# Depthwise convolution of 4 channel groups: one group as ScalarE products and GpSimd additions, 15 taps of another on TensorE, 78 taps on VectorE

## The reference

```python
def conformer_conv_group(a, gate, w_dw, b_dw, ln_g, ln_b):
    u = a * jax.nn.sigmoid(gate)
    k = w_dw.astype(u.dtype)[:, None, :]
    v = lax.conv_general_dilated(
        u, k, window_strides=(1,), padding=[(CONV_WIDTH - 1, 0)],
        dimension_numbers=("NWC", "WIO", "NWC"),
        feature_group_count=C_CONV) + b_dw.astype(u.dtype)
    v = layernorm(v, ln_g, ln_b)
    return jax.nn.silu(v)
...
        z = xn @ w_in[l] + b_in[l]
        a = z[..., :C_CONV]
        gate = z[..., C_CONV:2 * C_CONV]
        p = z[..., 2 * C_CONV:]
        y_conv = conformer_conv_group(a, gate, w_dw[l], b_dw[l], ln_g[l], ln_b[l])
        y_pool = multiscale_pool_group(p, w_pool[l], s_pool[l])
        y = jnp.concatenate([y_conv, y_pool], axis=-1)
        h = h + y @ w_out[l]
```

## Time and profile before

| | |
|---|---|
| median of 3 runs | 2058.88 us (2054.29 to 2060.63) |
| the profiled execution | 2058.82 us |
| its span in the profile | 2057.0 us |
| mean granted TensorE clock | 0.984 |
| PE busy | 1903.9 us, 93% of the span |
| DVE busy | 686.4 us, 33% |
| ACT busy | 467.6 us, 23% |
| POOL busy | 32.6 us, 2% |

### The profile page before, as it was taken

One profiled execution on the slowest core, in us unless ns is written; L12 is line 12 of the kernel. 1 busy time (PEld: TensorE's weight loads), 2 busy tenths in 40 slices (PEclk: granted clock), 3 DMA queues, 4 the chain that ended last, 5 costly groups with the idle time before them and its releaser, 6 DMA issues.

```text
span 2057.0 us, 20381 instructions
## 1 busy us (share of the span) xinstructions
PE 1903.9 (93%) x8678; PEld 1121.0 (54%) x8678; DVE 686.4 (33%) x944; ACT 467.6 (23%) x686; POOL 32.6 (2%) x41
## 2 busy tenths in 40 slices
PE   5989989999879999998888999988999999999998
PEld 5876766557644333343433334342344478888887
DVE  6474465376421110212011021201039742322234
ACT  5347545312211000010100001010030432222223
POOL 0000000000000000000000000000040000000000
PEclk9999999999989999999999999999999999999999
DMA  8211101386679999999999999999970105332311
GB/s 303 83 43 60 62 22 41 141 297 237 252 299 421 421 421 421 421 421 422 421 421 421 421 421 421 422 421 422 411 243 23 41 32 163 103 98 87 103 62 41
DMA packets 127551, 513.42 MB, mean 250 GB/s; under 512 B 7907, under 2 KB 62307, under 8 KB 77155
## 3 DMA queue, kind: packets, MB, share of 16 engines
q1 hardware_dynamic: 123088, 487.95, 59.8%
q10 hardware_dynamic: 4374, 24.18, 3.1%
HBM read 510.00 MB, written 2.10 MB: 249 GB/s over the span
## 4 chain that ended last, share of the span: by engine, by line
PE 69%; DMA 21%; DVE 6%; ACT 2%; issue 1%; SPq 0%; POOL 0%; ACTq 0%; DVEq 0%; POOLq 0%
PE ps L1147 10%; DMA work<-in_w_exp_up 9%; PE ps L1102 7%; DMA ring<-in_w_exp_up 7%; PE ps L1315 5%; PE ps L537 5%; PE ps L1275 4%; PE ps L1276 4%; PE ps L1274 4%; PE ps L553 3%; PE ps L555 3%; PE ps L1025 3%; PE ps L554 3%; PE ps L1128 2%; PE ps L736 2%; PE ps L1048 1%
## 5 line engine op out<-in xcount | busy, mean ns | idle before, releaser
L1102 PE MATMUL ps<-work 128*64 128x512 f32 x1208 | 329.6, 595 | 28.6 <-DMA work<-in_w_exp_up 28.4
L1102 PE MATMUL ps<-ring,work 128*64 128x512 f32 x712 | 218.5, 594 | 19.6 <-DMA ring<-in_w_exp_up 19.5
L1102 PEld LDWEIGHTS ps<-work 128*64 128x64 f32 x1208 | 104.5, 137 | 207.5 <-issue 150.2
L2250 DVE TENSOR_TENSOR work<-work,ps 64x512 f32<-64x512 f32 x64 | 44.3, 692 | 449.0 <-ACT work L1687 448.4
L1687 ACT ACTIVATE work<-ps 64x512 f32<-64x512 f32 x64 | 37.7, 589 | 563.4 <-PE ps L1102 563.4
L537 PE MATMUL ps<-work,ring 128*128 128x512 f32 x320 | 138.9, 592 | 0.7 <-issue 0.7
L1274 PE MATMUL ps<-xh,wh 128*128 128x512 f32 x352 | 137.0, 389 | 0.0
L1276 PE MATMUL ps<-xh,wl 128*128 128x512 f32 x352 | 136.9, 389 | 0.0
L1275 PE MATMUL ps<-xl,wh 128*128 128x512 f32 x352 | 136.9, 389 | 0.0
L1102 PEld LDWEIGHTS ps<-ring,work 128*64 128x64 f32 x712 | 67.7, 137 | 125.8 <-issue 88.6
L2383 DVE TENSOR_TENSOR wl<-ring,wh 128x2048 fp32r<-128x2048 f32 x33 | 75.6, 2292 | 179.9 <-ACT wh L1775 179.9
(11 more groups left out here) (344 smaller groups left out, 2583.7 us busy)
## 6 DMA issues: line engine op xcount, KB each, us to landing
work<-in_w_exp_down SPq DMA_DIRECT2D x78, 1024.0 KB, 26.5
work<-in_w_exp_gate SPq DMA_DIRECT2D x76, 1024.0 KB, 26.8
work<-in_w_exp_up SPq DMA_DIRECT2D x75, 1024.0 KB, 27.0
ring<-in_w_exp_up SPq DMA_DIRECT2D x45, 1024.0 KB, 27.1
ring<-in_w_exp_gate SPq DMA_DIRECT2D x44, 1024.0 KB, 26.7
ring<-in_w_exp_down SPq DMA_DIRECT2D x43, 1024.0 KB, 27.0
ring<-in_w_in SPq DMA_DIRECT2D x27, 1024.0 KB, 6.3
work<-in_ada_w ACTq DMA_DIRECT2D x16, 1024.0 KB, 6.1
```

Of the source, the lines that this page charges most:

```text
L1102: i = e.matmul(PS[64 * gu:64 * gu + 64, fb, :], at(XET + 128 * k + 64 * z, 64), flat(key)[:, 512 * fb:512 * fb + 512], start=(k == 0), sto ...
```

## The change

`DVE_TAPS = 16` is the number of taps of group 1 that stay on VectorE.

- Group 3 leaves TensorE. ScalarE makes each of its 31 products, tap 0 with the bias straight into `CV + 1536`, the others into four rooms of 512 columns (`tap_room`) used in turn. GpSimd adds tap 1 to tap 30 to the sum, one after the other. `cv_m` counts the products and `cv_g` what GpSimd has done: first the weight tiles, then the additions. A product of tap k above 4 waits for addition k - 4.
- Group 1: taps 0 to 15 stay on VectorE, taps 16 to 30 are made on TensorE in bank 6, after dense blocks 8 and 9. VectorE adds the bank to its own sum as its 79th step. GpSimd makes 15 weight tiles.
- On TensorE, dense blocks 8 and 9 now stand ahead of the taps and block 10 ahead of the mean. On ScalarE the third `pool_in` now stands ahead of the squares, and the products stand behind the sigmoids.
- `pool_window` has an additional wait for the window before it.

```diff
+        def tap_room(k):
+
+            return at(DG + 2048 + 512 * (k % 4), 512)
+
+        CV_G = 31 - DVE_TAPS + 30
...
             glu(3, 1, 2, 0)
-            e.wait_ge(s["gl_u"], 1)
+            pool_dense(8, 3, 5)
+            pool_dense(9, 2, 5)
+            e.wait_ge(s["gl_u"], 4)
             e.wait_ge(s["pads"], 1)
             e.wait_ge(s["x_ca"], 63)
-            for k in range(31):
-                e.wait_ge(s["dg"], k + 1)
-                p = e.matmul(bank(6), at(DG + 128 * k, 128), at(U + 542 * 3 + k, 512), start=(k == 0), stop=(k == 30))
+            for k in range(DVE_TAPS, 31):
+                e.wait_ge(s["cv_g"], k - DVE_TAPS + 1)
+                p = e.matmul(bank(6), at(DG + 128 * (k - DVE_TAPS), 128), at(U + 542 + k, 512), start=(k == DVE_TAPS), stop=(k == 30))
             p.then_inc(s["cv_pe"], 1)
-            pool_dense(8, 3, 5)
-            pool_dense(9, 2, 5)
+            pool_dense(10, 1, 4)
             e.wait_ge(s["x_ym"], 32)
             for i in (3, 2, 0, 1):
                 if i == 3:
-                    e.wait_ge(s["cv_a"], 1)
+                    e.wait_ge(s["cv_g"], CV_G)
                 else:
-                    e.wait_ge(s["cv_d"], {2: 44, 0: 78, 1: 93}[i])
+                    e.wait_ge(s["cv_d"], {2: 44, 0: 78, 1: 79}[i])
                 p = e.matmul(bank(4), cst("o512"), at(CV + 512 * i, 512), start=(i == 3), stop=(i == 1))
             p.then_inc(s["ln_pe"], 1)
-            pool_dense(10, 1, 4)
...
+            def tap_3(k):
+
+                w = at(O_VEC + VEC["wdw"][0] + 93 + k, 1)
+                if k == 0:
+                    e.wait_ge(s["gl_u"], 1)
+                    e.wait_ge(s["pads"], 1)
+                    e.activation(at(CV + 1536, 512), at(U + 542 * 3, 512), ACT.Identity, bias=vcol("bdw", 3), scale=w).then_inc(s["cv_m"], 1)
+                    return
+                if k > 4:
+                    e.wait_ge(s["cv_g"], 31 - DVE_TAPS + k - 4)
+                e.activation(tap_room(k), at(U + 542 * 3 + k, 512), ACT.Copy, scale=w).then_inc(s["cv_m"], 1)
...
                 e.activation(at(TP + 512 * m, 512), bank(2 * m % 4), ACT.Sigmoid, bias=vcol("bin", 4 + i)).then_inc(s["gl_sg"], 1)
+                for k in range(*((0, 5), (5, 13), (13, 21), (21, 31))[m]):
+                    tap_3(k)
...
-            conv((0, 14, 31), (1, 0, 17))
-            conv((1, 17, 31))
+            conv((0, 14, 31), (1, 0, DVE_TAPS))
+            e.wait_ge(s["cv_pe"], 1)
+            e.wait_ge(s["cv_d"], done[1])
+            e.tensor_tensor(at(CV + 512, 512), at(CV + 512, 512), bank(6), ALU.add).then_inc(s["cv_d"], 1)
...
-            for k in range(31):
-                e.tensor_scalar(at(DG + 128 * k, 128), ident, at(O_VEC + VEC["wdw"][0] + 93 + k, 1), None, ALU.mult).then_inc(s["dg"], 1)
+            for k in range(DVE_TAPS, 31):
+                e.tensor_scalar(at(DG + 128 * (k - DVE_TAPS), 128), ident, at(O_VEC + VEC["wdw"][0] + 31 + k, 1), None, ALU.mult).then_inc(s["cv_g"], 1)
+            v = at(CV + 1536, 512)
+            for k in range(1, 31):
+                e.wait_ge(s["cv_m"], k + 1)
+                if k > 1:
+                    e.wait_ge(s["cv_g"], 31 - DVE_TAPS + k - 1)
+                e.tensor_tensor(v, v, tap_room(k), ALU.add).then_inc(s["cv_g"], 1)
```

More of the change, by code:

```diff
@@ L22 @@
 FT = 22
+DVE_TAPS = 16
 CST = {}
@@ L187 @@
     "x_g x_oh x_xa x_xd x_ow x_ot x_oc x_gu x_sl x_hd x_ht x_hc x_dn x_ym x_cb x_ca "
-    "fx_h fx_l fw_h fw_l pads dg i2_pe gl_sg gl_u cv_pe cv_a cv_d pw_in pw_o po_pe po_y ln_pe dv sqv ln_a y_d y_a "
+    "fx_h fx_l fw_h fw_l pads i2_pe gl_sg gl_u cv_pe cv_g cv_m cv_d pw_in pw_o po_pe po_y ln_pe dv sqv ln_a y_d y_a "
     "o2_pe o2_x sx_h sx_l fs_h fs_l ff_pe ff_s ff_m hs_h hs_l dn_pe dn_e fin_x fin_a fin_o"
@@ L1236, in o2_free @@
                 elif u == 4:
-                    e.wait_ge(s["cv_a"], 1)
+                    e.wait_ge(s["cv_d"], 79)
                 elif u == 5:
@@ L1725, in _ @@
                 e.activation(at(TP + 512 * m, 512), bank(2 * m % 4), ACT.Sigmoid, bias=vcol("bin", 4 + i)).then_inc(s["gl_sg"], 1)
+                for k in range(*((0, 5), (5, 13), (13, 21), (21, 31))[m]):
+                    tap_3(k)
             o2_hi(2)
             o2_hi(3)
-            e.wait_ge(s["cv_pe"], 1)
-            e.activation(at(CV + 1536, 512), bank(6), ACT.Identity, bias=vcol("bdw", 3)).then_inc(s["cv_a"], 1)
             def pool_in(u, g, n):
@@ L1741, in _ @@
             pool_in(9, 2, 10)
+            pool_in(10, 1, 11)
             for i in range(4):
@@ L1746, in _ @@
                 e.activation(at(TP + 512 * i, 512), at(CV + 512 * i, 512), ACT.Square).then_inc(s["sqv"], 1)
-            pool_in(10, 1, 11)
+            e.wait_ge(s["cv_pe"], 1)
             pool_out(11, 3)
@@ L1750, in _ @@
             e.wait_ge(s["ln_pe"], 2)
-            e.wait_ge(s["cv_pe"], 1)
-            e.wait_ge(s["cv_d"], 93)
+            e.wait_ge(s["cv_d"], 79)
             e.activation(at(U, 512), bank(5), ACT.Ln, bias=vec("eps5")).then_inc(s["ln_a"], 1)
@@ L2344, in pool_window @@
                 e.wait_ge(s["pw_in"], 4 - g)
+                if g < 3:
+                    e.wait_ge(s["pw_o"], 3 - g)
                 e.wait_ge(s["pads"], 2)
```

## The result

The changed kernel takes 2064.1 us (median of 7 runs, 2062.27 to 2065.01) beside 2057.01 us for the kernel before (7 runs, 2054.29 to 2060.74, the three given above among them). The ratio is 1.0032, with a 95% interval of 1.0022 to 1.0041, so it is slower, by 4.5 to 8.4 us. The profiled execution took 2064.1 us for a span of 2062.3, against 2058.82 and 2057.0 before: 5.3 us more. The forecast was 2065.3.

The account below looks back on a forecast made before the run. TensorE ends last before the Ln, VectorE's path 0.6 us behind. VectorE's first pool window at 1601.3 + 20.6 = 1621.9 puts the Ln 6.8 us later, cut to 6.4: 2058.9 + 6.4 = 2065.3 us, range 2053 to 2071.

Parts of the forecast that it names:

- What bounds the kernel: Up to the Ln, TensorE ends last; alone it can give back at most 0.6 us, beyond that VectorE must give too.
- VectorE left alone: Without contention from GpSimd, VectorE's first pool window would start at 1601.3 instead of 1612.31.
- The price: Taps and additions take turns, 1.72 us a pair; 21 additions beside VectorE's taps cost it 20.6 us, against 11.0 saved.
- Who goes first: Additions alternate with all taps, ending near 1584, or enter only between dependent taps, ending near 1622; sum hardly changes.
- 4.52 us row: Earlier-trace row: a GpSimd instruction of 0.6 us stood behind two VectorE instructions in a row, though already waiting.
- Downstream: After the pool windows, subtractions, squares, pool copies and table load put the Ln at 1635.5, 6.8 us later, cut to 6.4.
- The clock: TensorE's restart at clock 0.50 after idling, full about 3.5 us after work resumed, costs 1.7 us, hidden in its taps.
- Rival 1: VectorE's taps don't contend with GpSimd's additions: Ln 12.0 us earlier, 2046.9 us; chance 0.12.
- Rivals 2 and 3: A turn costs VectorE only 0.4 us, 2053.5, chance 0.08; or full durations, 2.01 us a pair, 2071.8, chance 0.07.
- Slower: Whole kernel measurably slower than before: chance 0.47, made of 0.40 from the forecast's case and 0.07.
- the same one: Whole kernel not measurably different from before: chance 0.41, made of 0.33 from the forecast's case and 0.08.
- the bound: For the whole kernel, about 0.3% (6.2 us) is what a measurement can tell from no change, at 2065.1 us.

Follow-up runs that it names:

- half run: The changed kernel with only additions 1 to 15 of group 3 on GpSimd, all products kept: 2051.26 us beside 2059.11 for the kernel before.
- PSUM version: VectorE's running sums in PSUM banks instead of SBUF: in the changed kernel 2047.59 us, in the kernel before 2058.73, each beside 2059.11.

## Why the prediction was right

- **What bounds the kernel, and that VectorE has to give too.** Right. TensorE gave 13.7 us of taps and then stood for 11.95 us (forecast 13).
- **VectorE left alone.** 1601.3 forecast, 1601.17 in the run without additions.
- **The price.** 20.6 us forecast for 21 additions, 19.5 measured (that is 0.93 each). A pair of tap and addition takes 1.67 us instead of the 1.72 that I put together from the earlier trace rows. The half run gives 0.90 to 0.96 for an addition, where I had 0.93 beside dependent taps. As forecast, nine additions began before 1546.2; the tenth, for which I cut the 6.8 us to 6.4, came at 1547.04. The mechanism and its price come from two rows of another stage that had nothing to do with a convolution; that is what made the sign of the forecast right.
- **Who goes first.** Here I left two ways open, and measured is the one that I had derived from the Trainium skill, "SBUF — State Buffer", "Who interferes with whom". The last addition ends at 1584.06, the forecast by that page was 1584, by the 4.52 us row 1622. The row was a poor guide: it is one instruction of another kind. The page's other half, that the first holds the ports for its whole instruction, does not fit the GpSimd instruction with one operand: it is 1.59 us long and cost the taps 0.32 to 0.43. Here the measurement decides. That the order changes the sum little was only argued; no run had the other order.
- **Downstream.** The Ln came 5.66 us later, forecast 6.8, cut to 6.4. 1.1 us of the difference is the price above. The Ln waits for ScalarE's queue and not for the variance sum, as forecast.
- **The clock.** This term was mis-sized. The taps of TensorE after the pause took 15.88 us; in the run without additions, which has no pause, they took 13.04. That is 2.8 us and not 1.7. It is hidden. Block 10 ended at 1621.16, 0.4 us after VectorE's last step of the convolution (1620.11 + 0.67), and not before it as forecast; but the mean was done near 1624.7, before the pool windows that stand ahead of the subtractions (1627.6).

The windows of 2 us of the changed kernel show it (columns as in the earlier trace rows):

```profile
1596.00:1598.00 2.00, 0.00 (x0) 0.50 0.00 0
1598.00:1600.00 2.00, 1.42 (x2) 0.50 0.00 0
1600.00:1602.00 2.00, 2.00 (x3) 0.50 0.00 0
1602.00:1604.00 2.00, 2.00 (x4) 0.50 0.00 0
1604.00:1606.00 2.00, 2.00 (x6) 0.97 0.00 0
```

The engine works from 1598.6 on and has its full clock only from about 1604, 5.4 us later, where the earlier trace rows had made me expect 3.5; why it took longer here isn't shown. Half the clock for 5.4 us costs 2.7.

- **The rivals.** Rival 1 (no contention) is what the PSUM version has, and it came out 11.5 us below the kernel before, where 12.0 were worked out for it, so its arithmetic was right and its condition not met. Rivals 2 and 3 are excluded by 19.5 us for some 21 additions.

Slower had a chance of 0.47 and the same one of 0.41; the measured 0.32% lies just beyond the bound between them. On which side it fell is luck: 7.1 us between the medians is beyond the 6.2 us of the bound, and the 5.3 us of the traces is not.

## What to carry to other kernels

Before elementwise work is given to GpSimd, look at what VectorE does at that time. If both read two operands from SBUF, they take turns, and of GpSimd's 1.27 us for 512 columns VectorE pays 0.9 to 1.0. Instructions with one operand in SBUF were not always free of it either. If VectorE's running sum fits a free PSUM bank, its pace is the same and the two run side by side; here this small edit turned 0.3% slower into 0.5 to 0.6% faster. To see the contention in a profile, look for instructions that are longer than their kind, not for waits: there are none.

## What the runs showed of the hardware

- Taps and additions with two SBUF operands each: VectorE and GpSimd alternate at 1.67 us a pair, both in dependent taps and in taps that follow each other without a gap; no wait appears in the trace, the durations grow.
- A tap with one operand in SBUF and one in PSUM (0.75 us) isn't slowed, and hardly slows GpSimd (additions 1.40 us apart instead of 1.37). Whether it writes to PSUM or to SBUF made no difference. In a mixed sequence the SBUF tap paid 0.36 us.
- A VectorE tensor_scalar of tap 0 with one operand, from SBUF to SBUF, took 0.92 and 1.48 us beside the additions and 0.54 without them. With its result in PSUM it took 0.81 us with and without additions (the PSUM version of each kernel). No run was made to find out why.
- On GpSimd a tensor_scalar of 128x512 with one SBUF operand and a scalar per partition took 1.56 us, more than the addition of two operands (1.27), and cost VectorE 0.43 us beside alternating taps and 0.32 beside dependent ones.
- TensorE at half clock after a pause of 12 us needed 5.4 us of work until the granted clock was full again.
